# Expert 0's rows transposed by one-hot products, and the 64 first slots of every expert computed on 64 array columns at a time

## The reference, cut to what matters

```python
def moe_swiglu(h, w_router, w_gate, w_up, w_down):
    t = h.reshape(B * S, Dm)                        # 256 x 1024
    logits = (t @ w_router).astype(jnp.float32)
    top_vals, top_idx = lax.top_k(logits, TOP_K)    # TOP_K = 2 of N_EXPERTS = 8
    top_w = jax.nn.softmax(top_vals, axis=-1)
    gates = jnp.sum(jax.nn.one_hot(top_idx, N_EXPERTS) * top_w[..., None], axis=1)
    for e in range(N_EXPERTS):
        ye = swiglu(t, w_gate[e], w_up[e], w_down[e])   # 1024 -> 2816 -> 1024
        out = out + gates[:, e:e + 1] * ye
```

## Time and profile before

| | us |
|---|---|
| median of 3 runs (1048.09 to 1050.11) | 1048.44 |
| the profiled execution's own time | 1048.1 |
| its span, in which all times of the trace are given | 1046.3 |
| PE busy (matmuls) | 1022.9 |
| PEld busy (weight loads) | 578.9 |
| DVE busy | 270.5 |
| ACT busy | 250.7 |
| POOL busy | 54.3 |

### The profile page before, as it was taken

One profiled execution on the slowest core, in us unless ns is written; L12 is line 12 of the kernel. 1 busy time (PEld: TensorE's weight loads), 2 busy tenths in 40 slices (PEclk: granted clock), 3 DMA queues, 4 the chain that ended last, 5 costly groups with the idle time before them and its releaser, 6 DMA issues.

```text
span 1046.3 us, 22297 instructions
## 1 busy us (share of the span) xinstructions
PE 1022.9 (98%) x9903; PEld 578.9 (55%) x9903; DVE 270.5 (26%) x418; ACT 250.7 (24%) x426; POOL 54.3 (5%) x159
## 2 busy tenths in 40 slices
PE   8999999999999899999999999999999999999985
PEld 7987888888998654444433334444444444443321
DVE  7677545446677410000000000000000000000022
ACT  7766534344775200000000000000000000000021
POOL 4000000000101000001001000001001000100200
PEclk9999999999999999999999999999999999999998
DMA  8488556542638899999999999999999999999994
GB/s 290 175 264 275 195 175 201 186 160 97 213 112 299 293 366 361 420 418 359 397 420 408 419 418 408 418 419 401 399 419 419 402 419 419 406 418 418 418 406 166
DMA packets 125149, 347.24 MB, mean 332 GB/s; under 512 B 7368, under 2 KB 40176, under 8 KB 125056
## 3 DMA queue, kind: packets, MB, share of 16 engines
q1 hardware_dynamic: 119760, 331.64, 82.0%
q0 software_dynamic: 4560, 13.41, 3.8%
q10 hardware_dynamic: 736, 0.80, 0.2%
HBM read 341.10 MB, written 4.72 MB: 331 GB/s over the span
## 4 chain that ended last, share of the span: by engine, by line
PE 93%; DMA 3%; DVE 2%; issue 1%; SPq 1%; ACT 1%; DVEq 0%; ACTq 0%; POOLq 0%
PE ps L2011 29%; PE ps L2064 14%; PE ps L2015 10%; PE ps L1543 9%; PE ps L1545 9%; PE ps L1544 9%; PE ps L2069 5%; DMA ring<-in_moe_w_down 2%; PE ps L2026 1%; DMA gains<-tok_rows,tok_row 1%; PE ps L2099 1%; DMA raw_gu<-in_w_in 1%; SPq L831 0%; PE ps L1550 0%; PE ps L1932 0%
## 5 line engine op out<-in xcount | busy, mean ns | idle before, releaser
L2011 PE MATMUL ps<-ring,xg 128*32 128x512 f32 (+1 forms) x3072 | 380.0, 550 | 2.6 <-DMA ring<-in_moe_w_gate 1.6
L2064 PE MATMUL ps<-ring,moe_ht 128*32 128x512 f32 x1408 | 177.3, 593 | 2.7 <-DMA ring<-in_moe_w_down 2.7
L2015 PE MATMUL ps<-ring,xg 128*32 128x256 f32 x2048 | 176.2, 379 | 0.0
L2011 PEld LDWEIGHTS ps<-ring,xg 128*32 128x32 f32 x3072 | 110.6, 110 | 99.7 <-issue 47.3
L2015 PEld LDWEIGHTS ps<-ring,xg 128*32 128x32 f32 x2048 | 73.2, 110 | 146.6 <-issue 146.6
L1543 PE MATMUL ps<-hi_gu,xt_hi 128*128 128x512 f32 (+1 forms) x352 | 132.3, 376 | 1.3 <-DVE lo_gu L2257 1.1
L1545 PE MATMUL ps<-hi_gu,xt_lo 128*128 128x512 f32 (+1 forms) x352 | 129.1, 367 | 0.0
L1544 PE MATMUL ps<-lo_gu,xt_hi 128*128 128x512 f32 (+1 forms) x352 | 129.0, 367 | 0.0
L1438 ACT ACTIVATE moe_silu<-ps 128x512 f32<-128x512 f32 (+1 forms) x24 | 13.3, 553 | 333.8 <-PE ps L2015 275.3
L2701 DVE COPY moe_ht<-ps 128x256 f32<-128x256 f32 (+1 forms) x18 | 7.1, 394 | 295.5 <-PE ps L2037 295.5
L2069 PE MATMUL ps<-ring,moe_ht 128*32 128x256 f32 x1056 | 81.2, 379 | 0.0
(11 more groups left out here) (326 smaller groups left out, 879.5 us busy)
## 6 DMA issues: line engine op xcount, KB each, us to landing
ring<-in_moe_w_down SPq DMA_DIRECT2D x88, 1024.0 KB, 16.5
ring<-in_moe_w_gate SPq DMA_DIRECT2D x56, 1024.0 KB, 17.6
ring<-in_moe_w_up SPq DMA_DIRECT2D x56, 1024.0 KB, 17.9
ring<-in_moe_w_gate SPq DMA_DIRECT2D x40, 768.0 KB, 15.3
ring<-in_moe_w_up SPq DMA_DIRECT2D x40, 768.0 KB, 14.2
raw_gu<-in_dense_w_gate SPq DMA_DIRECT2D x22, 512.0 KB, 3.9
raw_gu<-in_dense_w_up SPq DMA_DIRECT2D x22, 512.0 KB, 4.9
raw_d<-in_dense_w_down SPq DMA_DIRECT2D x11, 1024.0 KB, 4.9
```

What stands on the lines that cost most here:

```text
L2011: last = pe.matmul(ps[tile(q), (B_GATE, B_UP)[part], 0:w // 2], xg[:, rows_at, k, tile(g)], weights[:, h * w // 2:(h + 1) * w // 2], start ...
L2015: last = pe.matmul(ps[tile(q), (B_GATE_B, B_UP_B)[part], 0:FC], xg[:, rows_at, k, A_SLOTS:SLOTS], weights[:, q * FC:(q + 1) * FC], start=k ...
L2064: last = pe.matmul(ps[tile(q), B_YA, :], moe_ht[:, at:at + 32], weights[:, h * 512:(h + 1) * 512], start=start, stop=stop)
```

## The change

1. Expert 0's rows are no longer gathered and transposed. PE makes `xg` for p = 0 straight from the token rows that are in SBUF (`rows`, tokens on the partitions) and the one-hot rows: for each block of 128 features, `rows` block (stationary, 128x128) times one-hots (96 moving columns), added over the two token tiles (`pick_rows`). It stands between `all_piece(2, 1)` and `all_piece(3, 1)`. `find_rows` for expert 0, the copy of its token numbers and POOL's gather go. `xg` moves to another place in SBUF, since `rows` is now read while `xg` is written.
2. In `gate_up` and `down` the A part uses two tiles of 64 array columns (all 64 slots) instead of four of 32, with the same moving columns for each. The B part stays in tiles of 32.

```diff
@@ first_chunk @@
                 find_places()
-                all_piece(1, 1, lambda: find_rows(0, range(1)))
+                all_piece(1, 1)
                 all_piece(2, 1)
-                all_piece(3, 1, turn_first)
-
-            def turn_first():
-                pe.wait_ge(counted, 1)
                 for part in range(2):
-                    turn_picked(0, part)
+                    pick_rows(part)
+                all_piece(3, 1)
+
+            def pick_rows(part):
+                pe.wait_ge(*((counted, 1) if part else (onehots_ready, 1)))
+                for k in range(4):
+                    at = slice((part * 4 + k) * P, (part * 4 + k + 1) * P)
+                    for t in range(TT):
+                        last = pe.matmul(ps[:, B_XG0[part], k * SLOTS:(k + 1) * SLOTS], rows[:, t, at],
+                                         onehots[:, t, 0, 0:SLOTS].bitcast(F32), start=t == 0, stop=t == TT - 1)
+                last.then_inc(picked_turned, 1)
@@ gate_up @@
-                    for q in range(4):
-                        h, g = divmod(q, 2)
-                        last = pe.matmul(ps[tile(q), (B_GATE, B_UP)[part], 0:w // 2], xg[:, rows_at, k, tile(g)],
+                    for h in range(2):
+                        last = pe.matmul(ps[half_tile(h), (B_GATE, B_UP)[part], 0:w // 2], xg[:, rows_at, k, 0:A_SLOTS],
                                          weights[:, h * w // 2:(h + 1) * w // 2], start=k == 0, stop=k == KT - 1)
@@ down @@
-                    for q in range(4):
-                        h, g = divmod(q, 2)
-                        at = a_at(p, c, b) + 32 * g
-                        last = pe.matmul(ps[tile(q), B_YA, :], moe_ht[:, at:at + 32], weights[:, h * 512:(h + 1) * 512],
+                    for h in range(2):
+                        at = a_at(p, c, b)
+                        last = pe.matmul(ps[half_tile(h), B_YA, :], moe_ht[:, at:at + A_SLOTS], weights[:, h * 512:(h + 1) * 512],
                                          start=start, stop=stop)
@@ POOL @@
             pool.wait_ge(tok_row_ready, 1)
-            gather_picked(0)
-            pool.wait_ge(tok_row_ready, 2)
-            pool.wait_ge(picked_turned, 2)
             gather_picked(1)
@@ find_slots (DVE) @@
-                dve.wait_ge(tok_row_mm, 1)
-                dve.tensor_copy(tok_row[:, 0:1], ps[:, B_PLACES, 8 * E:8 * E + 1]).then_inc(tok_row_ready, 1)
```

More of the change, by code:

```diff
@@ L169, in b_rows, with half_tile @@
         return slice(0, width(p, c) // FC * B_SLOTS)
+    def half_tile(h):
+        return slice(A_SLOTS * h, A_SLOTS * (h + 1))
     def tile(q):
@@ L274, in build_trunk @@
         x_res = sb("x_res", [P, TT, D])
-        any_rows = ExitStack()
-        xg = sb("xg", [P, 2, KT, SLOTS], at=any_rows)
-        any_rows.close()
         rows = sb("rows", [P, TT, D])
@@ L290, in build_trunk @@
         gains1 = sb("gains1", [P, D])
+        behind_mixing = ExitStack()
+        xg = sb("xg", [P, 2, KT, SLOTS], at=behind_mixing)
+        behind_mixing.close()
         gains2 = sb("gains2", [P, D])
@@ L1832, in find_places, with find_rows @@
                 last.then_inc(counts_mm, 1)
-            def find_rows(n, some):
-                pe.wait_ge(onehots_ready, n + 1)
-                for e in some:
+            def find_rows():
+                pe.wait_ge(onehots_ready, 2)
+                for e in range(1, E):
                     for t in range(TT):
@@ L2045, in down @@
                     pe.wait_ge(picked_ht_ready, 1)
-                    pe.wait_ge(tok_row_ready, 2)
+                    pe.wait_ge(tok_row_ready, 1)
                 else:
@@ L2090, in turn_picked @@
             def turn_picked(p, part):
[L2091 to L2096, removed]
+                cap = CAPS[p]
+                pe.wait_ge(picked_loaded, p * 16)
+                pe.wait_ge(xg_ready, 2 * p + part)
+                if has_b(p - 1):
+                    pe.wait_ge(ht_b_ready, b_chunk_of(p - 1, part) + 1)
                 for k in range(4):
                     at = slice((part * 4 + k) * P, (part * 4 + k + 1) * P)
-                    last = pe.transpose(ps[:, b, k * cap:(k + 1) * cap], picked[0:cap, at], ident[0:cap, 0:cap])
+                    last = pe.transpose(ps[:, B_XG, k * cap:(k + 1) * cap], picked[0:cap, at], ident[0:cap, 0:cap])
                 last.then_inc(picked_turned, 1)
@@ L2108, in experts @@
                         if (p, c) == (0, 0):
-                            find_rows(1, range(1, E))
+                            find_rows()
                             pick_hidden()
@@ L2652, in copy_tokens @@
             def copy_tokens():
-                dve.wait_ge(tok_row_mm, 2)
+                dve.wait_ge(tok_row_mm, 1)
                 dve.tensor_copy(tok_row[:, 1:E], ps[:, B_PLACES, 8 * E + 2:10 * E].rearrange("p (e c) -> p e c", c=2)[:, :, 0]
```

## The result

| | median us | runs | ratio to before, 95% interval |
|---|---|---|---|
| before | 1048.26 (1047.83 to 1050.11) | 4 | |
| changed | 1155.01 (1152.92 to 1156.14) | 4 | 1.1014 [1.0995, 1.1032] |

A forecast was written before the change was run, and what follows sets the result against it. The prediction took PE to bound the kernel, with the DMAs close behind. From the profiled 1048.1 us it summed 1048.1 - 2.9 - 5.3 + 120.0 = 1159.9, predicting 1160 us in a range of 1118 to 1172.

The forecast's parts named there:

- The bound: In experts with B slots, PE is busy for all of the 90.60 us, so added PE time counts one for one.
- Streaming on 64 columns costs the same: In the A part, two tiles side by side take two passes, 0.86 us as before, so streaming changes by nothing.
- The third rival: A's two tiles don't overlap fully: three passes instead of two, 223 us more, 1383 us in all; chance 0.02.
- Two changes of tile size in a group, at 0.13 and 0.165 us: In each group, A to B costs 0.13 us (420 times) and B to A 0.165 us (390 times).
- the term of 120.0 us: Cost of all tile-size changes in the experts: 54.6 + 64.4, and 1.0 for first A loads after whole-array work.
- The waits for weights go: In the last expert, the 5.3 us that PE waited for weights go, as the ring is full when p = 7 begins.
- The DMAs: Weight loading in B-slot experts: DMAs fall to some 315 GB/s, and SP waits for PE much more.
- Part 1: Before the experts, picking expert 0's rows on PE instead of gathering them starts the experts 2.9 us earlier.
- The three terms: The parts of the sum: -2.9 us before the experts, -5.3 for waits for weights, +120.0 for tile-size changes.
- The case with no price: Rival: changes between 64 and 32 columns in the groups cost nothing, 1045.2 us, or up to 1048; chance 0.08.

The follow-up runs named there:

- turns of 8 on 64 columns: The changed kernel with up to 8 blocks of A and then up to 8 of B, instead of A and B in turn: 1051.54 us, ratio 1.0024.

## Why the prediction was right, step by step

- **The bound.** PE without a gap in the B-slot experts: held, before and after.
- **Streaming on 64 columns costs the same.** Held. The expert without B slots is at its old time but for six groups of p = 1, and turns of 8 on 64 columns are 92.7 us against 90.8. The third rival's A part of 1.28 us isn't there; A takes 1.01, change included.
- **Two changes of tile size in a group, at 0.13 and 0.165 us.** Right in kind, and the count too: the changed kernel's trace has 420 changes from 64 to 32 and 389 back, where I counted 420 and 390. The sum of 0.295 measured 0.289, as 0.15 in the distance from A to B and 0.14 in that from B to A. That looks the other way round than my 0.13 and 0.165, because the exposed first loads of A lengthen A's own distance and those of B its own. Over the stage the term of 120.0 us is 116.2: the experts begin 1.73 us earlier than in the profile before (364.59, now 362.86) and the last chunk's `gate_up` of p = 7 begins 114.47 later (1001.25, now 1115.72). Of the 3.8 us too much, 420 x 0.006 = 2.5 are the price rounded up; the other 1.3 have no row of their own.
- **The waits for weights go.** Right, and too small: -5.3 against -7.4 (114.47 falls to 107.06 between there and the first closing product). I took the view's idle time as the whole cost of the ten waits; each costs some 0.2 us more, as the rows in the last section show.
- **The DMAs.** Held: SP's queue waits far longer for the B products that give ring pieces back, 512 us in all instead of 217, and the DMAs move 322 GB/s where I said 315.
- **Part 1.** -2.9 against -3.15. The pick took 3.49 us, not 3.84: its 32 records take 0.109 us each, while L1901's figure of 0.117 came from only 16, whose first step is 0.165 us and the others 0.112.
- **What wasn't in the sum.** The changed kernel's profile is 1.4 us late before the changed code, a spread between executions. With it the terms give -3.15 + 116.2 - 7.4 + 1.4 = 107.1, the 1142.30 - 1035.24 of the traces, from which they are read; the medians differ by 106.75.
- **What the closeness is worth.** 1160 against 1155. The three terms missed in the same direction, 0.25 + 3.8 + 2.1 = 6.15 us together, and the 1.4 us of spread hid a part of it. The price between 64 and 32 was carried over from other changes of tile size; that it has the same size was a chance taken, and the run bore it out.

The rule quoted from the Trainium skill (TensorEngine Tiling (Array Packing), "Key Properties": a change of tiling mode drains TensorE) is borne out for the step between 64 and 32 columns, which no row of before showed. The records of an A part's first pass last 643 ns where 592 is the usual (0.05 us of exposed loads), and with this and 0.01 us of stagger taken off, B starts 0.09 us late; with 0.025 and 0.02 taken off, A starts 0.09 late after B, as after the changes to and from 128 in the earlier trace rows. The trace shows the late starts, not what goes on in the array meanwhile. The case with no price, the strongest rival, would have given groups of 1.29 us.

## What to carry to other kernels

Keep one tile size through an inner loop, even at twice the instructions: here four tiles of 32 columns stream as fast as two of 64 (0.43 us a pass), while each pair of changes between the sizes costs 0.29 us. Where two sizes are needed, do all of one and then all of the other, and watch what is released later for it. Count changes, not instructions; and read distances between starts, since the busy times of the lines that slow down don't show the loss.

## What the runs showed that I had not expected

A wait of TensorE costs more than its idle time: ten waits for weights with 5.3 us of idle time cost 7.4 us. Two waits in the last expert before, then the same products in the changed kernel without one (timelines of PE):

```profile
1003.60 1.50 PE L2011 MATMUL ps<-ring,xg 128*32 128x384 f32 x16 [0.87 <-DMA ring<-in_moe_w_gate]
1005.44 1.50 PE L2011 MATMUL ps<-ring,xg 128*32 128x384 f32 x16 [0.34 <-DMA ring<-in_moe_w_gate]
```
```profile
1115.72 5.33 PE L2016 MATMUL ps<-ring,xg 128*64 128x384 f32 x32
1120.99 0.66 PE L2031 MATMUL ps<-ident,moe_hidden 128*128 128x128 f32 x4
```

Without a wait two blocks take (1120.99 - 1115.72) / 4 = 1.32 us; from 1003.60 to 1005.44 are 1.84, 0.52 more, of which the view calls 0.34 idle. Its idle time begins at the modelled end of the last record (1003.60 + 1.50), not at the time when the next start was due (1003.60 + 1.32).

And the 4.0 us wait for the gather had a second price of 1.6 us in the low clock after it (0.55 in the 3.6 us before the experts), more than the 1.3 that I had put to the six matmuls alone, because the transposes ran at it as well (1.18 us instead of 0.66).
